# A two-block transformer kernel: a place of its own for the output products' last unit, splits a unit ahead, and scan reads and attention end in another order

## What is computed

```
def reference(x, ..., w_in, w_out, w_gate_up, w_down, c_2, ada_w_2, ..., w_out_2, w_ffn_in_2, w_ffn_out_2):
    # block 1: h = x + rms(mixer(rms(x))), mixer = sparse attention (8 heads) and a gated MLP, then @ w_out
    #          h = h + rms((silu(gate) * up) @ w_down),  gate, up = rms(h) @ w_gate_up
    # block 2: shift, scale, gate = silu(c) @ ada_w + ada_b   (6 rows of 1024)
    #          mix = (sigmoid(g_a) * attention @ w_o_attn + sigmoid(g_b) * ssd_scan @ w_o_ssd) @ w_out
    #          x = x + gate_m * rms(mix);  x = x + gate_f * rms(swiglu(rms(x) * (1 + scale_f) + shift_f))
```

## Time and profile before

| | us |
|---|---|
| median of three runs | 959.17 |
| the profiled execution, around all | 958.45 |
| its span, first to last instruction | 956.7 |
| TensorE busy | 939.4 (98%) |
| VectorE busy | 660.8 (69%) |
| ScalarE busy | 539.4 (56%) |
| GpSimd busy | 234.3 (24%) |

### The profile page before, as it was taken

One profiled execution on the slowest core, in us unless ns is written; L12 is line 12 of the kernel. 1 busy time (PEld: TensorE's weight loads), 2 busy tenths in 40 slices (PEclk: granted clock), 3 DMA queues, 4 the chain that ended last, 5 costly groups with the idle time before them and its releaser, 6 DMA issues.

```text
span 956.7 us, 15380 instructions
## 1 busy us (share of the span) xinstructions
PE 939.4 (98%) x5665; PEld 801.9 (84%) x5665; DVE 660.8 (69%) x1098; ACT 539.4 (56%) x956; POOL 234.3 (24%) x235
## 2 busy tenths in 40 slices
PE   9999999999999999999999999999999999999997
PEld 8987777888887898999978899986688878888786
DVE  5765676777785768965678766777966767755453
ACT  6677675444443667844556456567864664544443
POOL 5304102111113140399932144330200111000100
PEclk9999999999999999999999999999999999999999
DMA  9755347789887813751049666551344778665561
GB/s 285 227 169 176 113 155 256 238 281 281 281 287 241 257 45 111 205 150 43 24 140 343 199 177 184 169 176 67 111 154 159 237 243 252 190 187 193 192 219 67
DMA packets 131352, 179.00 MB, mean 187 GB/s; under 512 B 8124, under 2 KB 96910, under 8 KB 131280
## 3 DMA queue, kind: packets, MB, share of 16 engines
q1 hardware_dynamic: 120384, 144.53, 47.1%
q0 software_dynamic: 10304, 33.18, 11.4%
q10 hardware_dynamic: 592, 0.34, 0.1%
HBM read 176.90 MB, written 1.12 MB: 186 GB/s over the span
## 4 chain that ended last, share of the span: by engine, by line
PE 89%; DVE 4%; ACT 3%; DMA 2%; issue 1%; POOL 0%; SPq 0%; DVEq 0%; ACTq 0%
PE bank L1968 18%; PE bank L2047 17%; PE bank L2049 16%; PE bank L2048 16%; PE bank L2483 1%; PE bank L2479 1%; PE bank L2506 1%; PE bank L2220 1%; PE bank L1999 1%; DVE w_lo L1347 1%; PE bank L2414 1%; DMA w_raw<-in_w_down 1%; PE bank L2102 1%; PE bank L2201 1%; PE bank L2643 1%
## 5 line engine op out<-in xcount | busy, mean ns | idle before, releaser
L1347 DVE TENSOR_TENSOR w_lo<-w_raw,w_hi 128x1024 fp32r<-128x1024 f32 (+1 forms) x243 | 285.1, 1195 | 80.8 <-ACT w_hi L870 80.4
L870 ACT ACTIVATE w_hi<-w_raw 128x1024 fp32r<-128x1024 f32 (+1 forms) x262 | 266.2, 1038 | 115.8 <-PE bank L2049 69.9
L2047 PE MATMUL bank<-w_hi,h_hi 128*128 128x512 f32 x448 | 179.0, 400 | 0.3 <-DVE m_buf L1865 0.3
L2049 PE MATMUL bank<-w_hi,h_lo 128*128 128x512 f32 x448 | 174.8, 390 | 0.0
L2048 PE MATMUL bank<-w_lo,h_hi 128*128 128x512 f32 x448 | 174.3, 389 | 0.0
L1968 PE MATMUL bank<-h_hi,w_hi 128*128 128x256 f32 x432 | 124.5, 288 | 1.2 <-DVE h_lo L1510 1.0
L1968 PE MATMUL bank<-h_lo,w_hi 128*128 128x256 f32 x432 | 122.1, 283 | 0.0
L1968 PE MATMUL bank<-h_hi,w_lo 128*128 128x256 f32 x432 | 122.1, 283 | 0.0
L2047 PE MATMUL bank<-w_hi,ff_hi 128*128 128x512 f32 x272 | 107.6, 396 | 1.5 <-DVE w_lo L1347 1.0
L2048 PE MATMUL bank<-w_lo,ff_hi 128*128 128x512 f32 x272 | 106.0, 390 | 0.0
L2049 PE MATMUL bank<-w_hi,ff_lo 128*128 128x512 f32 x272 | 105.9, 389 | 0.0
(11 more groups left out here) (462 smaller groups left out, 1597.7 us busy)
## 6 DMA issues: line engine op xcount, KB each, us to landing
w_raw<-in_w_in SPq DMA_DIRECT2D x84, 512.0 KB, 3.6
ada_raw<-in_ada_w POOLq DMA_DIRECT2D x48, 512.0 KB, 6.2
w_raw<-in_w_gate_up SPq DMA_DIRECT2D x88, 256.0 KB, 5.2
w_raw<-in_w_ffn_in SPq DMA_DIRECT2D x88, 256.0 KB, 4.0
w_raw<-in_w_down SPq DMA_DIRECT2D x22, 512.0 KB, 6.3
w_raw<-in_w_ffn_out SPq DMA_DIRECT2D x22, 512.0 KB, 4.4
w_raw<-in_w_out SPq DMA_DIRECT2D x16, 512.0 KB, 3.6
w_raw<-in_w_o_ssd SPq DMA_DIRECT2D x16, 512.0 KB, 3.6
```

The costliest lines, as they stand in the source:

```text
L870: act.activation(high(u, n), w_raw[:, u % RING, 0:n], ACT.Copy).then_inc(hi_ready, 1)
L1347: return dve.tensor_tensor(dst, src, hi.bitcast(F32), ALU.subtract)
L2047: pe.matmul(out, x_hi[:, k, x], hi, start=start, stop=False, skip_group_check=True)
L2049: return pe.matmul(out, x_lo[:, k, x], hi, start=False, stop=stop, skip_group_check=True)
```

## The change

- `spare`: the last unit of product 0 and of product 2 (their eighth) gets its parts in `ff_hi[:, 0:4]` and `ff_lo[:, 0:4]`, not in its ring slot; `freed_at` skips it, and ScalarE's split of it waits as for held units.
- `product_end` and `boundary` of products 0 and 2 split one unit more at each place, on ScalarE and on VectorE: the last unit before the first squares, v before the second, v+1 and v+2 before the warm-up of the root and `square_m1`, v+3 before `square_x`. Product 1 keeps its order.
- `pool_held` keeps only the latent product's v+3. GpSimd no longer splits a unit at product ends 0 and 2; there VectorE does. What stood behind these splits in GpSimd's program, a row load (product 0, now behind a wait for the row loads before) and the `ada_w` chunk 10 (product 2), stands behind what came before.
- Attention: no units are split in the last pair; ScalarE does its exponentials in two halves with the copy of `pcT` between, reads the second bank of u behind them, warms the gelu table up before `mix_hi(0)` and does the gelu in two halves with a signal each. VectorE's additions of the block values go behind the last pair's scaling.
- Scan: ScalarE copies the gate before it splits, with a signal for each token half, and TensorE waits for the half that it overwrites.

VectorE's `product_end` and `boundary` change as ScalarE's do; they are left out here.

```diff
@@ -379,13 +379,14 @@
     pool_conv = range(s_xbc.u0 + 3, s_gb.u0, 2)
-    pool_held = tuple(st.u0 + 3 for st in NEXT)
+    spare = tuple(st.u0 + 7 for st in (s_wo, s_wo2))
+    pool_held = (s_lat.u0 + 3,)
     pool_lows = frozenset(u for part in (pool_held, pool_u, pool_lat, pool_topk, pool_conv) for u in part)
         prev = u - RING
-        while prev in held:
+        while prev in held or prev in spare:
             prev -= RING
@@ -393,6 +394,8 @@
             return lat_hi[:, u - s_lat.u0, 0:n]
+        if u in spare:
+            return ff_hi[:, 0:4, :].rearrange("p f s -> p (f s)")
         if u in held:
@@ -401,6 +404,8 @@
             return lat_lo[:, u - s_lat.u0, 0:n]
+        if u in spare:
+            return ff_lo[:, 0:4, :].rearrange("p f s -> p (f s)")
         if u in held:
@@ -772,7 +777,7 @@
         pool.wait_ge(h_lo_ready, H_MIX + 4)
-        split(pool_held[0])
+        pool.wait_ge(post_in, 16)
         load_row(post_rows[1], a["norm_ffn_post"], post_in)
@@ -795,7 +800,7 @@
         load_row(pre_rows[1], mod_dram[D:2 * D], pre_in)
-        split(pool_held[1])
+        split(pool_held[0])
         for u in pool_lat:
@@ -832,7 +837,6 @@
         load_row(pre_rows[2], mod_dram[4 * D:5 * D], pre_in)
-        split(pool_held[2])
         for c in (10, 11):
@@ -863,7 +867,7 @@
                 act.wait_ge(sums_out, 48)
-            elif u in held:
+            elif u in held or u in spare:
                 act.wait_ge(unit_used, s_wo.u0 + 2 if u < s_lat.u0 else s_wo2.u0)
@@ -940,9 +944,10 @@
             st = PRODUCTS[b]
-            split_to(st.u0 + len(st.ks) + 3)
+            more = 1 if b in (0, 2) else 0
+            split_to(st.u0 + len(st.ks) + 3 + more)
             square_m0(b, 0)
-            split_to(st.u0 + len(st.ks) + 4)
+            split_to(st.u0 + len(st.ks) + 4 + more)
             square_m0(b, 1)
@@ -955,11 +960,11 @@
                 link(ins)
-            split_to(v + 2)
+            split_to(v + 2 if b == 1 else v + 3)
             act.activation(warm[:, 2 + b:3 + b], eps, ACT.Sqrt)
             root_m(b, 0)
-            split_to(v + 3)
+            split_to(v + 3 if b == 1 else v + 4)
             square_x(b, 0)
@@ -1070,16 +1075,17 @@
-        def pair_exp(n):
+        def pair_exp(n, halves=(0, 1)):
             nk = P * (n % 2 + 1)
-            for half in range(2):
+            for half in halves:
                 act.wait_ge(max_ready, 2 * n + half + 1)
                                          bias=st1[:, n % 2, 0, i:i + 1], accum_out=st1[:, n % 2, 1, i:i + 1])
-            ins.then_inc(exp_ready, 1)
+            if halves[-1] == 1:
+                ins.then_inc(exp_ready, 1)
@@ -1103,14 +1109,21 @@
         for n in range(N_PAIR + 1):
-            if n < N_PAIR:
+            if n < N_PAIR - 1:
                 split_to(filled(n, 0) + 3)
-                if n in (5, 7):
-                    read_u((n - 5) // 2)
+                if n == 5:
+                    read_u(0)
                 pair_exp(n)
+            if n == N_PAIR - 1:
+                pair_exp(n, (0,))
+                act.wait_ge(cmp_mm, 4)
+                act.activation(pcT[:, :, :], bank[6][:, 0:2 * P].rearrange("p (t q) -> p t q", t=TT), ACT.Copy
+                               ).then_inc(cmp_act, 1)
+                pair_exp(n, (1,))
+                read_u(1)
             if n >= 1:
                 pair_pT(n - 1)
-            if n < N_PAIR:
+            if n < N_PAIR - 1:
                 split_to(min(filled(n, 1) + 3, s_wo.u0 + RING))
@@ -1136,14 +1149,13 @@
                                pc[:, :, :, 0:NCMP].rearrange("p t h j -> p (t h) j"), ACT.Exp).then_inc(cmp_act, 1)
-            if n == 6:
-                act.wait_ge(cmp_mm, 4)
-                act.activation(pcT[:, :, :], bank[6][:, 0:2 * P].rearrange("p (t q) -> p t q", t=TT), ACT.Copy
-                               ).then_inc(cmp_act, 1)
             if n == 7:
+                act.activation(warm[:, 7:8], eps, ACT.Gelu_apprx_tanh)
                 mix_hi(0)
                 act.wait_ge(act_read, s_u.act0 + 2)
-                act.activation(zu[:, :, :], zu[:, :, :], ACT.Gelu_apprx_tanh).then_inc(zu_ready, 1)
+                for half in range(2):
+                    act.activation(zu[:, 2 * half:2 * half + 2, :], zu[:, 2 * half:2 * half + 2, :],
+                                   ACT.Gelu_apprx_tanh).then_inc(zu_ready, 1)
         mix_hi(2)
@@ -1280,14 +1292,13 @@
                                    bias=not_cum[:, 1, h:h + 1]).then_inc(dec_ready, 1)
-            if i in SCAN_UNITS:
-                split_to(s_gb.u0 + SCAN_UNITS[i])
             if i in GB_READ:
                 for t in range(TT):
-                    ins = act.activation(w_tok[:, t, 512 * c:512 * c + 512], bank[t][:, :], ACT.Copy)
-                ins.then_inc(gb_ready, 1)
+                    act.activation(w_tok[:, t, 512 * c:512 * c + 512], bank[t][:, :], ACT.Copy).then_inc(gb_ready, 1)
+            if i in SCAN_UNITS:
+                split_to(s_gb.u0 + SCAN_UNITS[i])
             if i >= 4:
@@ -1296,7 +1307,7 @@
             half = slice(512 * c, 512 * c + 512)
-            act.wait_ge(gb_ready, c + 1)
+            act.wait_ge(gb_ready, TT * c + TT)
             for t in range(TT):
@@ -1628,7 +1640,8 @@
                 break
-            split_to(filled(n, 0) + 3)
+            if n < N_PAIR - 1:
+                split_to(filled(n, 0) + 3)
             if n == 6:
@@ -1637,14 +1650,10 @@
                 pair_out(2)
-                dve.wait_ge(att_ready, 3)
-                dve.wait_ge(cmp_mm, 5)
-                dve.tensor_tensor(mix[:, 0:2, :], mix[:, 0:2, :], bank3[2], ALU.add)
-                dve.tensor_tensor(mix[:, 2, :], mix[:, 2, :], bank3[3][:, 0, :], ALU.add).then_inc(att_ready, 1)
             pair_scale(n)
                 pair_max(n + 1)
-            split_to(min(filled(n, 1) + 3, s_wo.u0 + RING))
+                split_to(min(filled(n, 1) + 3, s_wo.u0 + RING))
             if n == 4:
@@ -1655,9 +1664,13 @@
             if n == 7:
+                dve.wait_ge(att_ready, 3)
+                dve.wait_ge(cmp_mm, 5)
+                dve.tensor_tensor(mix[:, 0:2, :], mix[:, 0:2, :], bank3[2], ALU.add).then_inc(att_ready, 1)
+                dve.tensor_tensor(mix[:, 2, :], mix[:, 2, :], bank3[3][:, 0, :], ALU.add)
                 operand_lo(0, H_MIX, mix, 0)
-        dve.wait_ge(zu_ready, 1)
         for c in (2, 3):
+            dve.wait_ge(zu_ready, c - 1)
             dve.tensor_tensor(mix[:, chunk(c), :], mix[:, chunk(c), :], zu[:, 2 * c - 4:2 * c - 2, :], ALU.mult
@@ -2573,8 +2586,8 @@
                 pe.wait_ge(dve_read, s_gb.dve0 - 1 + q // 4)
-            if q == 16:
-                pe.wait_ge(gb_ready, 1)
+            if q in (16, 20):
+                pe.wait_ge(gb_ready, q // 4 - 3)
             if t == 0 and k % 2 == 0:
@@ -2584,8 +2597,8 @@
             j, t, kk = q // 4, q % 4 // 2, q % 2
-            if q == 0:
-                pe.wait_ge(gb_ready, 2)
+            if q in (0, 2):
+                pe.wait_ge(gb_ready, TT + 1 + q // 2)
             if q % 4 == 0:
...
```

## The result

The changed kernel takes 969.15 us, the median of 5 runs (967.41 to 970.09); the kernel before takes 959.17 (5 runs, 958.67 to 960.32). The ratio is 1.010, its 95% interval 1.0089 to 1.0112. Forecast were 961.7 us and a range up to 964.3. The sign was right; 2.5 us were forecast and 10.0 measured. In later comparisons the kernel before stood at 958.4 to 959.4 us; a second timing of the changed kernel, beside it, gave +8.97 us.

The account below looks back on a forecast made before the run. TensorE, busy 98% of the span, was taken as the bound, with 4.91 us of targeted waits. Scan and attention -0.75, first block -0.7 and second product end +4.0 gave +2.55: 961.7 us median, range 957.8 to 964.3.

Parts of the forecast that it names:

- Scan, -0.75: Scan reads: copying the gate before the split, with a signal per half, removes TensorE waits of 0.33 and 0.42 us.
- I take no cost: Scan: the split comes 1.08 us later, but TensorE needs that unit two gate steps later or more, so zero cost.
- Attention end, -1.2: Attention end: exponentials fill ScalarE's idle time, so the output product starts at about 116.95 instead of 118.12.
- First product end, +0.2 at the first turn, -0.93 at the second: First block: v+2 landing at 134.8 puts the first turn at 142.3; the second turn's wait goes; net -0.7 us.
- Second product end, L - 754.25 = +4.0: Second block's end: early ada_w loads delay v+2 and the squares behind its split; net +4.0 us, bounds +0.8 to +6.2.
- L: Landing time of v+2 at the second product end: 758.3 forecast, bounds 755.05 and 760.5.
- with half of 292/0.87 = 336 GB/s: Second product end: weights keep half the DMA rate beside the early loads, so their 1.8 MB take 10.7 us.
- the last unit lands about 1.3 us later: Second product end: the last unit's load is 1.3 us later; TensorE waits under 1 us, inside the same stall.
- 1.22 less: Second product end: waits of 0.83 us before the second turn and 0.39 us after the first turn go.
- more than half: Rival, second product end: the other queue's bursts delay v+2 to 760.5 or the last unit; +4.75, 963.9 us; chance 0.13.
- Spare time only: Rival, second product end: GpSimd's early loads take only what the weights leave; -0.65, 958.5 us; chance 0.30.
- the first block wins in full: Rival: row load finds engines free, first turn at 141.0, second block loses least; 957.2 us; chance 0.12.

Follow-up runs that it names:

- ada_late: Changed kernel with GpSimd's ada_w loads at the second product end held back until v+3's low part is there: 960.56 us, +2.13 over the kernel before.
- row_late: ada_late with the first product end's row load (norm_ffn_post, 512 KB) also held back until v+3's low part is there: 957.89 us, -0.84 against the kernel before.
- kept_busy: Changed kernel with 9 and 15 unused TensorE matmuls before the second product end's last-unit and first-turn waits: 965.67 us, +7.24 over the kernel before.
- changed_again: Changed kernel unaltered, timed again on the chip of kept_busy_both: 967.72 us, +8.97 over the kernel before.
- before_ada_early: Kernel before with only the four loads of ada_w chunk 10 put ahead of GpSimd's split of v+3: 964.81 us, +6.38 over the kernel before.
- kept_busy_both: kept_busy with 9 more unused matmuls ahead of the first product end's first turn: 965.73 us, +6.98 over the kernel before.
- small_packets: Changed kernel with the four early ada_w loads of 512 KB issued as eight of 256 KB: 968.89 us, +9.50 over the kernel before.

## Why the prediction was wrong

**Scan, -0.75.** Right in size for the scan (-0.88). "I take no cost" for the later split was wrong: the 0.88 are already less a new wait of 0.23 us in the scan, and 0.51 us come back as two small waits behind it, so 0.37 is what is left.

**Attention end, -1.2.** Right: -1.25 from the same maxima.

**First product end, +0.2 at the first turn, -0.93 at the second.** The second was right (-1.05), by the mechanism named. At the first, v+2 landed at 135.75 and not 134.8, and the turn came 1.1 us after 142.3. But the path was another: ScalarE was free for v's split from 130.8 and waited for its load, landed at 132.84, which I hadn't looked at; when it came to v+2's split, that unit had been there for 0.1 us. The row load costs 0.75 of it, as ada_late and row_late show, and half a microsecond had come in before the attention. Net +0.24 in place of -0.7. With the scan, the changed kernel was 0.14 us ahead when it came to the second end, where the forecast had 1.45.

**Second product end, L - 754.25 = +4.0.** That the early `ada_w` loads make the weights late and the squares wait for them was right and is shown: these loads alone give +6.4, and holding them back takes 7 away. The unit was not the right one: the squares hung on v's landing at 757.64 and ScalarE's work behind it, and v+2 came 0.2 us before it was needed. That L still gives their start, 1.25 us later, is luck. This is the term that was mis-sized, in two ways.

First L: 760.46, where the forecast had 758.3 and the upper bound 760.5. The step that failed is "with half of 292/0.87 = 336 GB/s": the engines gave 384 to 397 GB/s, but the weights' queue moved 0.51 MB of 1.59 from 748 to 752, a third. The even halves of 741 to 748, which I took as agreeing with turns by packet, were even in bytes alone: 285 packets against 635. For the same reason "the last unit lands about 1.3 us later" was 2.9 us (752.60 against 749.68), and TensorE waited 2.27 us, not under 1. That wait lies in front of the same turn, so it isn't added. With L = 760.46 the forecast's own formula gives +6.2.

Second, the clock, which no term of the sum has. I noted that the granted clock was 1.00 in the kernel before and didn't ask what waits of 2 and 4 us would do to it. The stretch between the two turns took 10.14 us in place of 8.95, where the formula had 1.22 less: 2.4 us, and kept_busy measures 2.3. That is the price in this execution, with 6.8 us at the lower level there; in changed_again's, with 3.4 us, the turns are 8.73 us apart, 0.9 more than in kept_busy. Add 0.44 by which it was longer from v+2's landing to the turn than I had it (6.98 us against 1.2 + 5.34), and 6.2 + 0.44 + 2.4 = 9.04, the shift of the second turn.

The rival *more than half* had the share right and 963.9 us as its time; without the clock it too falls short. *Spare time only* is refuted by before_ada_early, *the first block wins in full* by the turn at 143.42.

## What to carry to other kernels

When work is taken out of a queue that also issues DMAs, list what it was holding back and look at what those transfers will run beside. Bound the share of a critical stream by less than half when another queue moves large transfers, and price a wait of TensorE of 2 us twice: the wait, and the time that may follow at half the clock. Look for the first unit that comes late, not only for the last one in the order. If the early transfer isn't needed early, one wait on the event that used to stand in front of it costs nothing; here it was worth about 7 us.

## What the runs showed of the hardware

**The clock fell behind some waits of TensorE of 1.8 to 5.1 us, and not behind others as long.** In the fourteen traces there are 19 waits of 2.0 us or more after the first 100 us; 11 go with a stretch at the lower level, 8 don't. Among them, waits of 2.27 and 3.72 us were followed by the lower level in the changed kernel; 2.47 (first end) was in ada_late, 2.27 (second end) in the same execution was not, and in before_ada_early neither 2.52 nor 3.60 was. In kept_busy_both it fell behind 1.78. In changed_again the first end's wait of 2.57 us was, where 2.77 in the first trace was not. And twice (row_late, 100 to 104 us, 0.62; small_packets at 100.4) it fell with no such wait near. An average over executions is needed for its price. The Trainium skill (TensorE: Matmul & The Clock Gate, HAM oscillation) describes a kernel that falls to 1.2 GHz at each wait for a DMA and reckons the loss as half of the slow time; by it 10.3 us slow would be 5.2 us lost, an estimate. The traces agree on the work (half of 10.3 us at a granted clock of one half) and not on the time: the 3.4 slow us of the first stretch lay in front of another wait, and only 2.3 us of time reached the end.

**The queue of the large transfers took more than half.** GpSimd's queue took 1.08 MB of 1.59 from 748 to 752 beside weights that ScalarE waited for. With row loads beside them (741 to 748) the halves had been even. What decides between the two is not shown. The DMA engines moved up to 400 GB/s with both queues full (before_ada_early, 748 to 752), and 331 GB/s with the weights alone at 95% of the engines' time (row_late, the same stretch).
